# Turning q, k, y1 and y0 by VectorE in 32x32 blocks with a pass through DRAM, instead of on TensorE

## The reference

```python
def pool_layer(x, norm_g, w_in, w_pool, pool_scale, w_out):
    h = rms_norm(x, norm_g)
    u, z = jnp.split(h @ w_in, 2, axis=-1)
    y = pool_mixer(u, w_pool, pool_scale) * jax.nn.silu(z)
    return x + y @ w_out
...
def moba_layer(x, norm_g, w_in, q_norm, k_norm, w_out):
    h = rms_norm(x, norm_g)
    q, k, v, z = jnp.split(h @ w_in, 4, axis=-1)
    q = rope(rms_norm(heads(q), q_norm))
    k = rope(rms_norm(heads(k), k_norm))
    v = heads(v)
    o = moba_attention(q, k, v).transpose(0, 2, 1, 3).reshape(B, S, D_INNER)
    return x + (o * jax.nn.silu(z)) @ w_out
```

## Time and profile before

| | us |
|---|---|
| median of 3 runs (431.88 to 432.15) | 431.96 |
| the profiled execution | 431.83 |
| its span, first to last instruction | 430.0 |
| PE busy | 423.4 (98%) |
| DVE busy | 284.7 (66%) |
| ACT busy | 231.0 (54%) |
| POOL busy | 131.1 (30%) |
| DMA queue of SP, share of 16 engines' span | 53.1% |

### The profile page before, as it was taken

How to read it: one execution, slowest core, us unless ns; L and a number is a source line. 1 busy time by engine, 2 the same in 40 slices (tenths; PEclk the granted TensorE clock), 3 DMA queues, 4 the chain that set the end, 5 groups by cost and what they waited for, 6 DMA issues and landing times.

```text
span 430.0 us, 5669 instructions
## 1 busy us (share of the span) xinstructions
PE 423.4 (98%) x2214; PEld 362.7 (84%) x2214; DVE 284.7 (66%) x354; ACT 231.0 (54%) x406; POOL 131.1 (30%) x97
## 2 busy tenths in 40 slices
PE   8999999999999999999999999999999999999997
PEld 8979898988888888888788888888888888888885
DVE  3868898779885544356664798447983579836532
ACT  5743653535454443578448765477654786546310
POOL 0078000000000000089904595055940559300000
PEclk9999999999999999999999999999999999999999
DMA  8987669563655747336833667236672355731002
GB/s 260 386 298 241 209 219 365 190 201 122 197 194 173 219 134 221 125 89 214 292 99 99 185 183 228 91 100 193 196 215 84 101 191 195 243 110 39 2 0 98
DMA packets 38026, 75.25 MB, mean 175 GB/s; under 512 B 1648, under 2 KB 1776, under 8 KB 38000
## 3 DMA queue, kind: packets, MB, share of 16 engines
q1 hardware_dynamic: 37280, 73.83, 53.1%
q10 hardware_dynamic: 720, 1.07, 0.8%
HBM read 73.84 MB, written 1.05 MB: 174 GB/s over the span
## 4 chain that ended last, share of the span: by engine, by line
PE 85%; POOL 7%; DMA 2%; DVE 2%; SPq 1%; ACT 1%; issue 1%; DVEq 0%
PE acc L579 23%; PE acc L581 22%; PE acc L580 22%; PE aux L634 4%; POOL wide L326 3%; PE acc L624 3%; PE acc L623 3%; PE acc L621 3%; DMA raw<-in_w_in_dram 2%; PE aux L718 2%; POOL k_s L319 1%; PE aux L725 1%; SPq L232 1%; PE aux L736 1%; PE aux L737 1%; PE aux L717 1%
## 5 line engine op out<-in xcount | busy, mean ns | idle before, releaser
L816 DVE TENSOR_TENSOR w_lo<-raw,w_hi 128x2048 fp32r<-128x2048 f32 x65 | 160.1, 2469 | 54.9 <-ACT w_hi L349 54.8
L349 ACT ACTIVATE w_hi<-raw 128x2048 fp32r<-128x2048 f32 x64 | 122.1, 1917 | 36.7 <-PE acc L581 25.7
L579 PE MATMUL acc<-w_hi,hT_hi 128*128 128x512 f32 x320 | 127.8, 399 | 1.0 <-DVE w_lo L816 1.0
L581 PE MATMUL acc<-w_hi,hT_lo 128*128 128x512 f32 x320 | 124.9, 390 | 0.0
L580 PE MATMUL acc<-w_lo,hT_hi 128*128 128x512 f32 x320 | 124.6, 389 | 0.0
L579 PEld LDWEIGHTS acc<-w_hi,hT_hi 128*128 128x128 f32 x320 | 60.1, 188 | 12.9 <-DVE w_lo L816 1.4
L581 PEld LDWEIGHTS acc<-w_hi,hT_lo 128*128 128x128 f32 x320 | 60.0, 188 | 12.9
L580 PEld LDWEIGHTS acc<-w_lo,hT_hi 128*128 128x128 f32 x320 | 60.2, 188 | 11.7
L579 PE MATMUL acc<-w_hi,aT_hi 128*128 128x512 f32 x160 | 63.7, 398 | 0.0
L581 PE MATMUL acc<-w_hi,aT_lo 128*128 128x512 f32 x160 | 62.4, 390 | 0.0
L580 PE MATMUL acc<-w_lo,aT_hi 128*128 128x512 f32 x160 | 62.3, 389 | 0.0
(11 more groups left out here) (125 smaller groups left out, 569.7 us busy)
## 6 DMA issues: line engine op xcount, KB each, us to landing
raw<-in_w_in_dram SPq DMA_DIRECT2D x46, 1024.0 KB, 5.4
raw<-in_w_out_dram SPq DMA_DIRECT2D x16, 1024.0 KB, 5.0
raw<-in_w_pool_dram SPq DMA_DIRECT2D x4, 1024.0 KB, 5.7
raw<-in_w_in_dram SPq DMA_DIRECT2D x8, 256.0 KB, 7.5
wide<-in_xT_dram ACTq DMA_DIRECT2D x4, 256.0 KB, 7.0
xs<-in_x_dram SPq DMA_DIRECT2D x1, 1024.0 KB, 7.8
out_dram<-ysb SPq DMA_DIRECT2D x4, 256.0 KB, 2.1
wide<-in_table_dram SPq DMA_DIRECT2D x1, 256.0 KB, 9.0
```

What stands on the lines that cost most here:

```text
L349: act.activation(w_hi[:, slot, :], raw[:, slot, :], ACT.Copy).then_inc(hi_made, 1)
L579: pe.matmul(a, shi, whi, start=first and k == 0, stop=False)
L581: ins = pe.matmul(a, slo, whi, start=False, stop=last and k == GK - 1)
L816: dve.tensor_tensor(w_lo[:, slot, :], raw[:, slot, :], w_hi[:, slot, :].bitcast(F32), ALU.subtract).then_inc(w_split, 1)
```

## The change

The turns of y0, of all q and k, and of y1 for groups 0 to 2 leave PE. x's turns and the last y1's stay.

- DVE transposes a 128x1024 tensor (tokens t, heads h) in 32x32 blocks (`blocks`, one instruction). SP then stores it to DRAM (512 KB), waits for that to land, and issues four loads of 128 KB, each of which brings the block rows of one quarter of the partitions back (`move_blocks`). The pieces are 256 elements, 1 KB.
- What comes back holds the transposed tensor with its 32-column blocks in the order (a, t, h, i). ACT's copy puts q in order (`lay_q`), PE reads k as it is, and the high and low parts of y0 and y1 are made by t.
- DVE does the whole rotary step (`rope`); POOL keeps only the powers (`norms`); ACT scales k (`scale_k`).
- The pooled scale is loaded as a row for all partitions into `xs` and multiplied into the gate by DVE, one instruction a group; x itself is loaded later, ahead of the third output granule's weights.
- SP's order of transfers, ACT's order at the end of a group (y1's high part now ahead of the gate's tanh) and DVE's order change accordingly.

```diff
+            def move_blocks(dst, blocks, between, times, stored, landed):
+                if times:
+                    sp.wait_ge(landed, MOVED * times)
+                sp.dma_start(between, blocks).then_inc(stored, 16)
+                sp.wait_ge(stored, 16 * (times + 1))
+                quadrants = between.rearrange("(a j) (b n) -> b j a n", j=Q, n=2 * P)
+                for b in range(P // Q):
+                    sp.dma_start(dst[b * Q:(b + 1) * Q, :].rearrange("j (a n) -> j a n", n=2 * P),
+                                 quadrants[b]).then_inc(landed, 16)
...
+                    if h == 1:
+                        move_y0(q)
+                    if (h, q) == (0, 2):
+                        sp.wait_ge(gate_scaled, GROUPS)
+                        sp.dma_start(xs[:, :, :], x[0].rearrange("(t p) n -> p t n", p=P)).then_inc(x_landed, 16)
                     load(q, w_out0_v[:, q * GK:(q + 1) * GK, h * COLS:(h + 1) * COLS], N_OUT0 + 4 * h + q)
...
+            for i in range(8 * GROUPS + 8):
+                g, j = divmod(i - 7, 8)
+                if i >= 7 and g < GROUPS:
+                    if j == 3:
+                        move_q(g)
+                    if j == 5:
+                        move_k(g)
+                    if j == 6 and g > 0:
+                        move_y1(g - 1)
...
             def y0_hi(g):
-                for b in range(2):
-                    turned_hi(aT_hi, HPG * g + 2 * b, 2 * (g % 2) + b, (y_turned, 2 * g + b + 1), y_hi, gain=2 * KD)
+                act.wait_ge(y0T_landed, MOVED * (g + 1))
+                for t in range(TT):
+                    act.activation(y_tiles(aT_hi, g, t), y0T(g, t), ACT.Copy).then_inc(y_hi, 1)
...
+            def scale_k(g):
+                act.wait_ge(k_rstd_made, g + 1)
+                for t in range(TT):
+                    for h in range(HPG):
+                        tile = k_s[:, t, h * HEAD_DIM:(h + 1) * HEAD_DIM]
+                        ins = act.activation(tile, tile, ACT.Copy, scale=k_rstd[:, t, h:h + 1])
+                ins.then_inc(k_scaled, 1)
...
                 w(7)
+                if attend:
+                    y1_hi(g - 1)
                 tanh_z(g, not attend)
-                if attend:
-                    y1_hi(g - 1)
-                qkT_out(g, 1)
...
-                if g > 0:
-                    turn_y0(g - 1)
...
-                    if j == 6:
-                        turn_qk(g, 0, first)
-                    if j == 7:
-                        if not first:
-                            turn_y1(g - 1, g)
-                        turn_qk(g, 1, first)
...
+            def blocks(dst, src):
+                return dve.transpose(dst.rearrange("p (b n i) -> p n b i", b=P // Q, i=Q),
+                                     src.rearrange("p t n -> p (t n)").rearrange("p (n b i) -> p n b i", b=P // Q, i=Q))
...
+            def rope(g, i):
+                if i == 0:
+                    dve.wait_ge(summed[0], g + 1)
+                else:
+                    dve.wait_ge(k_scaled, g + 1)
+                v4 = qk[i].rearrange("p t (h d) -> p t h d", h=HPG)
+                s4 = scratch[i].rearrange("p t (h d) -> p t h d", h=HPG)
+                for a, b in ((0, half), (half, 0)):
+                    tab = rope_tab[:, 2 * i + 1, :, a:a + half].unsqueeze(2).to_broadcast([P, TT, HPG, half])
+                    ins = dve.tensor_tensor(s4[:, :, :, a:a + half], v4[:, :, :, b:b + half], tab, ALU.mult)
+                chain.done(ins)
+                tab = rope_tab[:, 2 * i, :, :].unsqueeze(2).to_broadcast([P, TT, HPG, HEAD_DIM])
+                chain.done(dve.tensor_tensor(v4, v4, tab, ALU.mult))
+                chain.done(dve.tensor_tensor(qk[i], qk[i], scratch[i], ALU.add))
+                blocks(scratch[i].rearrange("p t n -> p (t n)"), qk[i]).then_inc(qk_blocked[i], 1)
...
+                rope(g, 0)
                 w(3)
...
-                rope_sum(g, 0)
+                rope(g, 1)
                 if attend:
                     head_out(g - 1, 3)
                 w(5)
+                if attend:
+                    y1_turn(g - 1)
                 w(6)
-                rope_sum(g, 1)
                 w(7)
                 gate_z(g)
```

More of the change, by code:

```diff
@@ L311, in norm_rope @@
                     pool.wait_ge(exp_made, HPG * (g - 1))
-                scaled = pool.tensor_tensor(q_rstd[:, g % 2] if i == 0 else k_rstd[:, :, :], qk_mean[:, i],
-                                            minus_half[:, :].rearrange("p (t h) -> p t h", t=TT), ALU.pow)
+                ins = pool.tensor_tensor(q_rstd[:, g % 2] if i == 0 else k_rstd[:, :, :], qk_mean[:, i],
+                                         minus_half[:, :].rearrange("p (t h) -> p t h", t=TT), ALU.pow)
                 if i == 0:
-                    scaled.then_inc(qk_scaled, 1)
-                else:
[L317 to L331, removed]
+                    chain.done(ins)
+                    pool.tensor_scalar(minus_rstd[:, g % 2], q_rstd[:, g % 2], -1.0, 1.0, ALU.mult,
+                                       ALU.mult).then_inc(qk_scaled, 1)
+                else:
+                    ins.then_inc(k_rstd_made, 1)
             for g in range(GROUPS):
-                norm_rope(g, 0)
-                norm_rope(g, 1)
+                norms(g, 0)
+                norms(g, 1)
         @block.scalar
@@ L435, in h1_hi @@
                     turned_hi(hT_hi, 4 * half + 2 * b, 2 * half + b, (h_turned, 2 * half + b + 1), h_hi, gain=KD)
-            for n in range(N_OUT0 + 4, N_OUT0 + 8):
+            for n in range(N_OUT0 + 5, N_OUT0 + 8):
                 static_hi(n)
@@ L549, in _ @@
                     probs_out(last, j - 1)
-            y1_hi(last)
+            y1_hi_last()
         @block.tensor
@@ L708, in scores @@
             def scores(g, h):
[L710 to L713 removed]
+                pe.wait_ge(qT_made, TT * (g + 1))
+                pe.wait_ge(qkT_landed[1], MOVED * (g + 1))
+                if HPG * g + h < 2:
+                    pe.wait_ge(h_split, 4)
                 else:
@@ L955, in h1_lo @@
                               gain=KD)
-            for n in range(N_OUT0 + 4, N_OUT0 + 7):
+            for n in range(N_OUT0 + 5, N_OUT0 + 7):
                 weight_lo(n, n % RING)
@@ L1006, in y1_lo @@
             def y1_lo(g):
-                for b in range(2):
-                    y1_lo_bank(g, b)
+                for t in range(TT):
+                    dve.wait_ge(y_hi, 8 + 2 * g + t + 1)
+                    dve.tensor_tensor(y_tiles(aT_lo, g, t), y1T[:, :, t].rearrange("p a h i -> p h a i"),
+                                      y_tiles(aT_hi, g, t).bitcast(F32), ALU.subtract).then_inc(y_split, 1)
             def layer1(g, attend):
```

217 lines of the change are left out of this document (126 added, 91 removed).

## The result

The changed kernel took 464.43 us (median of 4, 463.20 to 469.04; 432.01 before on the same chip): ratio 1.077, interval 1.072 to 1.082. Forecast were 439.0, and 419 to 447 as the range. It is slower, as forecast, but by 32 us and not by 7, and outside the range. The profiled execution took 463.2 us, its span is 461.2 (before 430.0).

What follows compares the result with a forecast made beforehand. PE (TensorE), busy 423.4 of 430.0 us, was taken as the bound. 431.8 - 13.9 = 417.9, plus 10.7 for y0 and 11.5 for y1 gave 440.1, less 1 for queueing: 439, range 419 to 447.

Steps and rivals of the forecast that it cites:

- What leaves PE, 13.9 us: PE's queue: 15 turns at 0.88 us go, 13.2 us, and with k's turn its wait of 0.7.
- Loads back 3.6: Each move's four loads of 128 KB: last leaves 1.4 us after the first, lands 2.1 later; bounds 2.5 and 5.
- rival 2: Loads back: a 1 KB piece takes as long as one of 2 KB, 1.3 us more per 512 KB; 448 us, chance 0.09.
- A store behind a weight load lands 1.3 us after it: SP's queue: a 512 KB store issued just behind a 1 MB load lands up to 1.3 us later.
- The weight load ahead lands in 5.2: SP's queue: a lone 1 MB load takes 5.2 us; the one ahead of y1's store was to land at 53.7.
- Each us after 55.5 is a us of idleness: Probs in layer 1: y1's lateness idles PE one for one, 3.4 us in two groups, 4.7 after the third, together 11.5.
- y0 10.7 us: Output granules: y0 cycles of 8.5 us in SP's queue make q = 3 start 10.7 us late; 1.4 without queueing.
- q and k hidden: Attention stage: moves of q and k priced 0; k is back at 50.4, its scores at 56, 5 us of cover.
- Scalings and strided scores at 0: Four gate scalings of 1.2 us in layer 0 (4.9 without cover) and scores reading k in 32-column runs, priced 0.
- "Minus 1": The sum: 1 us taken off 440.1 because the 1.3 us of queueing was held to be an upper bound.
- 1 (all hidden): Whole kernel: all moves are hidden, 418 to 421 us, chance 0.17.
- 3 (one place late): Either y0's or y1's delays remain, not both: 429, range 423 to 433 us, chance 0.19.

Runs made afterwards that it cites:

- experiment 3: Changed kernel with y0 and y1 turned by TensorE again, so only q and k move by way of DRAM: 423.92 us, 0.981 of the kernel before.
- 8: Changed kernel with y0 on TensorE, y1's move ahead of the weight load, y1's copies behind the next group's first exponential: 421.21 us, 0.975 of the kernel before.
- experiment 5: Changed kernel with all moves (stores and loads back of y0, q, k, y1) issued by GpSimd on its own queue: 501.99 us, 1.160 of the kernel before.
- Experiment 6: Changed kernel with y1's store and loads back ahead of the 1 MB weight load in SyncE's program: 445.31 us, 1.032 of the kernel before.
- experiment 4: Changed kernel with matmuls that nobody reads put where TensorE waits for y0 and y1: 461.14 us, 1.067 of the kernel before.
- experiment 11: Changed kernel, everything still moved, with y0's and y1's moves ahead of weight loads, x behind y0's, y1's copies later: 424.32 us, 0.983 of the kernel before.
- experiment 1: Changed kernel with y1 of groups 0 to 2 turned by TensorE again; y0, q and k still move: 437.18 us, 1.013 of the kernel before.
- 7: Changed kernel with y0's moves put ahead of weight loads and x's 1 MB load behind them: 456.85 us, 1.059 of the kernel before.
- 10: The kernel of experiment 3 with three pauses at the probs, TensorE running 28 matmuls that nobody reads in each: 452.92 us.

## Why the prediction was wrong, step by step

- **What leaves PE, 13.9 us: right.** Experiments 3 and 8 are what it gives, with turns put back: 424.1 and 421.4 worked out, 423.92 and 421.21 measured.
- **Block transpose 1.2 us: right** (1.24 in the row above). DVE's whole chain to y1 was right as well: done at 47.9 forecast, 273.7 - 226.2 = 47.5 measured.
- **Store on an empty queue 2.8: right** (2.7).
- **Loads back 3.6: short by 0.5 to 1.3.** From SP's 285.63 to ACT's 289.98 it is 4.35 us, 4.2 in the other two groups, and 4.1 to 4.9 for y0. The sum was short too: 1.4 and 2.1 are 3.5. This is rival 2's direction, mostly at less than its price of 1.3. The sentence of the Trainium skill on small DMAs that the prediction draws on ("Perfetto Trace Analysis", "DMA Optimizations") agrees in direction, but no run changed the length of the pieces alone.
- **A store behind a weight load lands 1.3 us after it: right** (the load 276.51 + 7.8 = 284.3, the store 285.6).
- **The weight load ahead lands in 5.2: wrong, and the larger part of y1's miss. This is the step that failed first.** 5.2 is a lone load. It stood behind k's pieces and took 7.8. k's own store stood behind two weight loads that q's move had held back, so that SP sent k's pieces until 276.5, 50.3 in the group's time, not 48.4. The prediction let each transfer wait for its neighbour only, and read the delay as an order within one queue; by experiment 5 another queue doesn't avoid it. Experiment 6 shows that this is the cause: with y1's store ahead of that load the kernel is 19 us faster. In the group's time: weight load landed at 58.1 (forecast 53.7), store 59.4 (55.3), pieces 63.7 (58.9).
- **Each us after 55.5 is a us of idleness: right within 1 us.** 63.7 gives 8.2, and 7.3 was measured; 7.1 and 7.9 in the others. The term of 11.5 us should have been some 22.
- **y0 10.7 us: met by the waits' 11.2, but by luck.** The prediction's 10.7 is the delay of q = 3 behind 137.5. It started at 151.9, 14.4 us late and not 10.7; 2.2 us of that delay PE spent at the low clock and some in the stops, so the waits show less. The second cycle took 11.1 us and not 8.5 (the other two 8.5 and 8.9), with a weight load behind the loads back once more, which took 8.0. The first store landed at 117.4 (forecast 117.0), but the working doesn't give it: 3 MB at 0.38 MB per us from 105.2 are gone at 113.1, not at 115.7. In the trace 3.5 MB took 12.1 us, 0.29 MB per us.
- **q and k hidden: right**, with 3 us of cover instead of 5 (k back at 279.1, its scores at 282.0). **Scalings and strided scores at 0: right**, by experiment 3.
- **The sum took PE's speed as constant: wrong.** There was no term for the clock, though the earlier trace rows only show a PE that never rests, and every wait was itself priced. The clock and the stops are worth 11.6 us, half of what lay between 439 and 464, and 10.4 of it is the clock's; y1's waits, 22.3 for 11.5, are the other half. This is how the time divides, not what mending either alone returns: experiment 4 kept the clock up and got 2 to 3 us back.
- **"Minus 1", taken off for an upper bound of queueing, went the wrong way.** The bound wasn't one: it took the load ahead as alone.
- **The rule that 128x128 transposes belong on TensorE** (the Trainium skill, "VectorE: DVE Perf Modes", "Rules for kernel authors") names the sign. But the runs don't bear it out as the reason: where PE is the bound and the moves are issued in time, the way over DVE and DRAM beats the turns: 421.2 with y0 on TensorE and 424.3 with all moved, against 432.

Of the rivals, 1 (all hidden) is what experiment 11 nearly reaches, by order; 3 (one place late) did not come about.

## What to carry to other kernels

Work taken from the bounding engine is worth its time only if what replaces it comes in time: lay out every transfer in order of issue, each behind all that is still on its way, in whichever queue, and let the moves that someone waits for go ahead of prefetches that nobody waits for yet. Put the consumer of a round trip behind the work that doesn't need it. And where a forecast has TensorE idle for several us, add the clock: here 1.5 to 2.8 us for each idle stretch of 7 to 8.5 us. It adds to the time only where PE is the bound behind the wait, and not the next transfer, as experiment 4 shows.

## What the runs showed beside that

- The two kernels without new waits are also steady, with runs within 0.2 us (experiments 3 and 8). With waits left they lay 2 to 6 us apart. I take it that landings scatter and that PE waits out each scatter; no run separates this.
- A load back of 128 KB takes 2.8 us from SP's queue and 5.7 from GpSimd's, although that queue's packets are 3.1 KB on the mean (15.73 MB in 5040).
- Short waits cost some clock too, but not always. It fell behind waits of 2.5 us (changed kernel), 3.3 (experiment 1), 2.1 and 2.4 (6), 2.3 and 2.8 (7) and 2.1 (10). It stayed up behind 3.0 (changed kernel), 2.1 (6), and 2.1 and 1.9 (10).
- Open: what in GpSimd's queue takes that long; and what decides in which of these short waits the clock falls.
